# v of the gate by column blocks, u after it, and a sum with relu in one VectorE instruction

## Chip, cores and metric

One Trainium2 chip runs the same program on its 8 cores; each core computes one of the 8 sequences. There is no exchange between cores. The metric is the device time of the slowest core in microseconds (us), as a median over runs.

## What is computed

For each sequence x of 2048 positions with 1024 channels, two layers, each a token mixer and an MLP, each sub-layer followed by LayerNorm(alpha x + f(x)):

```
h = gelu(x @ w_in + b_in); u, v = h[..., :2048], h[..., 2048:]
v = layer_norm(v, v_g, v_b)                       # over 2048 channels
v = einsum('gts,bnsgc->bntgc', mask(w_s), v) + b_s  # 128 positions, 8 groups
mixer A = (u * v) @ w_out + b_out
mixer B = (b * causal_conv3(c * h)) @ w_out,  [b, c, h] = x @ w_in
MLP     = square(relu(x @ w1)) @ w2               # hidden 4096
```

Layer 0 uses mixer A, layer 1 mixer B.

## The kernel before

The sequence is done in two halves (h = 0, 1) of 1024 positions: eight token tiles (tt) of 128. For each half the stages are the gate (`gate_mixer`, mixer A), an MLP, `conv_mixer`, and a second MLP. `xres` holds the residual in fp32, `xT` the normalized input transposed in fp16, `H` 16 chunks of 128 hidden channels by 1024 positions. Weights are read as fp32 and cast to fp16 by the DMAs that GpSimd (POOL) issues: "ws" buffers (8, one block of 1024 x 128) and "wq" buffers (17, 512 x 512 each). SyncE (SP) issues x, rows of constants, transposes and the output.

In the gate, u comes out transposed (channels on partitions) in 16 blocks `u_block(fc, tb)` of eight matmuls for each 512 positions (L440), with the bias in ACT's gelu (L869). v comes out with positions on partitions: `v_tile(tt)` makes four products of 512 channels (`gemm_T`, L582), each ended by a ninth matmul that adds the bias from a small table `gc` (L585), then gelu (L906), statistics (L908), the reciprocal root on POOL, the normalization on ACT (L918) and the gain (L924, on POOL or VectorE). `sgu(tt)` mixes: ACT copies a bias into a bank (L932), four matmuls of 128 x 128 add the mixed v (L939), VectorE multiplies with u into H (L946). The order is: eleven u blocks, the tables (`init_gate`), v of tile 0, five u blocks, then v of tile tt + 1 with the mixing of tile tt. Then w_out is loaded into eight wq buffers, the first two token tiles are multiplied plainly, and the rest goes through `strassen_T`, a two by two block scheme with seven products, whose weight sums (`block_sums`, L411) take six more buffers.

`strassen_F` does the same for the first MLP product: 13 groups in each MLP call, six further blocks of a call's first half are plain or halved. Of a group's four results two are in PSUM banks, and two are the sum of a bank f and an fp32 tile ("k2" pool, VectorE L512). `square` then takes the relu on ACT into a k2 tile (L1043) and the square from there into H on VectorE (L1048) or ACT (L1049).

The order on each engine is made ahead by a planner (`Prog.schedule`): every operation has an engine or two, a duration and a program position; at each step the planner takes for each engine the operation that can start first (position decides within 0.05 us) and of these the earliest. Buffers of a pool are given in program order. Of a paced DMA it counts the bytes issued and lets at most 1.6 MB be under way: the DMA that moves the window gets waits on those that fell out of it. VectorE, ACT, POOL and SP run their lists strictly in order.

Of the kernel before, what the change touches and what calls it, by code (L numbers as in the profile page):

```python
# [8 lines left out]
FH = mybir.dt.float16  # L9
# [16 lines left out]
PATIENCE = 0.8  # L26
DMA_WINDOW = 1.6e6
# [18 lines left out]
class Prog:  # L46
# [60 lines left out]
    def schedule(self):  # L107
# [15 lines left out]

        def offer(op):
            for e in op.either or (op.eng,):
                cand[e].append(op)
# [6 lines left out]
        issued, total, low = [], 0, 0  # L133
        done = 0

        def start_of(op, e):
            t = max(op.ready, eng_free[e])
            if op.is_dma and op.paced:
                j = low
# [13 lines left out]
        while done < len(ops):  # L153
            best = None
            for e in ENGINES:
# [15 lines left out]
                if best is None or key < best[0]:  # L171
                    best = (key, e, op)
            assert best is not None, "no operation can start: a pool is held"
# [41 lines left out]
            for u in op.users:  # L215
                u.nleft -= 1
                lat = SEM_LAT if u.eng != op.eng or op.is_dma or u.either else 0.08
                u.ready = max(u.ready, op.end + lat)
                if u.nleft == 0:
                    offer(u)  # L220
# [122 lines left out]
def build_nc():  # L343
    nc = bass.Bass("TRN2", target_bir_lowering=False, dynamic_dma_scratch_size=4096)
# [14 lines left out]
    with es:  # L359
# [126 lines left out]
        def strassen_F(w, S, epilogue):  # L486
# [19 lines left out]
            epilogue(0, 0, a, True)  # L506
            for s, last in ((v, False), (u, True)):
                if last:
                    prod(b, W(w1, 1), SX(2), False)
                    epilogue(1, 0, b, True)  # L510
# [63 lines left out]
        def gemm_T(tt, wqs, hchunks=True, bias_q=None, gc=None):  # L574
            bk = vt("ps")
            A = H if hchunks else xT
            nk = 4 * len(wqs)

            def mm(e):
                ins = None  # L580
                for kc in range(nk):
                    ins = e.matmul(bk.buf[:], A[:, kc, tt * 128:(tt + 1) * 128], wqs[kc // 4].buf[:, kc % 4, :],  # L582
                                   start=(kc == 0), stop=(kc == nk - 1 and bias_q is None))
                if bias_q is not None:
                    ins = e.matmul(bk.buf[:], gc.buf[:, 1, bias_q * 128:(bias_q + 1) * 128], gc.buf[:, 0, :],  # L585
                                   start=False, stop=True)
                return ins
            rd = list(wqs) + ([("H", kc, tt) for kc in range(nk)] if hchunks else [("xT", tt, c) for c in range(8)])
            if bias_q is not None:
                rd += [(gc, 0), (gc, 1)]  # L590
            add("pe", mm, reads=rd, writes=[bk], dur=(nk + (bias_q is not None)) * T_MM)
            return bk

        def transpose_pe(xb, tt, gb=None):
            for q in range(2):
# [31 lines left out]
                add("act", None, reads=[bk, "gbT"], writes=wr, either={"act": (on_act, 1.55), "dve": (on_dve, 1.2)})  # L627

        def transpose_tiles(xbs, t0, gb=None):
# [8 lines left out]
            for q in range(2):  # L638
# [8 lines left out]
                def affine_act(e, q=q):  # L647
# [6 lines left out]
                    either={"act": (affine_act, 4 * (0.2 + n * 0.107)), "dve": (affine, 4 * (0.07 + n * 0.04))})  # L654
# [100 lines left out]
        def load_x(h, tt):  # L755
            r0 = (h * NT + tt) * 128
            add("sp", lambda e: e.dma_start(out=xres[:, tt, :], in_=x_ap[r0:r0 + 128, :]),
                writes=[(("xres", tt), 0), (("xres", tt), 1)], dma=("xr", tt), nbytes=128 * 4096, dur=0.06,
                paced=h > 0 or tt >= 4)
# [26 lines left out]
        def init():  # L786
# [12 lines left out]
            gc = vt("wt")  # L799
            clear_gc(gc)  # L800
# [3 lines left out]
            for bk in [vt("ps") for i in range(8)]:  # L804
                for i in range(2):
                    add("pe", lambda e, bk=bk: e.matmul(bk.buf[:], ones_bf[:], gc.buf[:, 0, :], start=True, stop=True),
                        reads=["ones", (gc, 0)], writes=[bk], dur=0.43)
            return gc

        def clear_gc(gc):  # L810
            add("dve", lambda e: e.memset(gc.buf[:, 0, :], 0.0), writes=[(gc, 0)], dur=0.3)

        def init_gate(gc):
# [4 lines left out]
            hi, lo, b = vt("k2"), vt("k2"), vt("k2")  # L818
            add("sp", lambda e: e.dma_start(out=b.buf[0:8, :], in_=bass.AP(rows_d, 9 * 1024, [[512, 4], [0, 2], [1, 512]])),
                writes=[b], dma=("c3", gc.seq), nbytes=16384, dur=0.06)  # L820
            add("dve", lambda e: e.tensor_copy(gc.buf[0:8, 0, :], b.buf[0:8, :]), reads=[b], writes=[(gc, 0)], dur=0.4)
            add("dve", lambda e: e.tensor_copy(hi.buf[0:8, :], gc.buf[0:8, 0, :]), reads=[(gc, 0)], writes=[hi], dur=0.4)
            add("dve", lambda e: e.tensor_tensor(lo.buf[0:8, :], b.buf[0:8, :], hi.buf[0:8, :], op=ALU.subtract),
                reads=[hi, b], writes=[lo], dur=0.7)
            add("dve", lambda e: e.tensor_tensor(hi.buf[0:8, :], hi.buf[0:8, :], lo.buf[0:8, :], op=ALU.subtract),
                reads=[hi, lo], writes=[hi], dur=0.7)
# [320 lines left out]
```

## Time and profile before

| | |
|---|---|
| median of 3 runs | 1458.36 us (1454.5 to 1460.49) |
| the profiled execution | 1464.58 us |
| its span on the slowest core (core 4) | 1463.0 us; all cores 1429.4 to 1463.0 |
| TensorE matmul (PE) | 1403.1 us busy, 96% |
| VectorE (DVE) | 1069.8 us, 73% |
| ScalarE (ACT) | 702.4 us, 48% |
| GpSimd (POOL) | 240.9 us, 16% |
| the chain that ended last | PE 71%, DMA 16%, issue 4%, ACT 4%, DVE 3% |

The profile follows one execution. "L440" is a line of the kernel. Matmuls are pipelined, so the busy time of one is longer than what it takes of PE's stream; the distance from one start to the next shows that. Idle time is put down to what ended it.

### The profile page before, as it was taken

The numbers are of one execution on the slowest core, as the hardware profiler recorded it, in microseconds if no ns is written. First come the engines' busy times: TensorE is split into PE (matmuls) and PEld (weight loads), VectorE is DVE, ScalarE is ACT, GpSimd is POOL, SyncE is SP. The second block draws the span as 40 slices with busy tenths as digits, with TensorE's granted clock in tenths as the row PEclk, the third lists the DMA queues.
The fourth block names the chain that finished last, engine by engine and source line by source line (L and its number), as shares of the span: only waits on it lengthen the run. The fifth ranks groups of instructions, "written<-read, shape, count | busy, mean of one in ns | idle before, by whom it ended". The sixth has DMA issues, their size and how long they took to land.

```text
span 1463.0 us, 23273 instructions; the slowest of 8 cores (1429.4 to 1463.0 us)
## 1 busy us (share of the span) xinstructions
PE 1403.1 (96%) x6988; PEld 665.9 (46%) x6988; DVE 1069.8 (73%) x2055; ACT 702.4 (48%) x1221; POOL 240.9 (16%) x422
## 2 busy tenths in 40 slices
PE   7999999998999998999998999999999999999996
PEld 3444445443446444443443444454444644544443
DVE  3257877887788677967681679779687876788777
ACT  2347457426463276336343574671474424751642
POOL 1125212111001101112011242121120111111100
PEclk7999999999999999999999999999999999999999
DMA  8999027856526739678988951293883364775702
GB/s 182 138 135 146 1 44 122 138 88 108 93 45 87 110 59 142 94 120 126 133 175 199 186 79 15 44 153 64 147 133 69 63 110 80 118 121 83 120 1 115
DMA packets 101138, 153.14 MB, mean 105 GB/s; under 512 B 52744, under 2 KB 52744, under 8 KB 101016
## 3 DMA queue, kind: packets, MB, share of 16 engines
q0 software_dynamic: 46608, 112.74, 50.6%
q1 hardware_dynamic: 54408, 38.91, 11.8%
q8 instruction: 59, 0.97, 0.3%
q14 instruction: 63, 0.52, 0.1%
HBM read 244.42 MB, written 8.39 MB: 173 GB/s over the span
## 4 chain that ended last, share of the span: by engine, by line
PE 71%; DMA 16%; issue 4%; ACT 4%; DVE 3%; POOL 1%; SPq 0%; DVEq 0%; POOLq 0%; ACTq 0%
PE ps L454 44%; PE ps L440 17%; PE ps L582 8%; DMA wq<-wbig 8%; DMA ws<-wsm 4%; DMA xT<-xb 2%; ACT xb L673 1%; ACT xT L650 1%; DMA wq<-x 1%; PE ps L939 1%; DMA xres<-x 1%; DMA sc<-rows 1%; DMA wt<-wsT 1%; PE ps L585 1%; ACT ps L932 1%
## 5 line engine op out<-in xcount | busy, mean ns | idle before, releaser
L440 PE MATMUL ps<-xT,ws 128*128 128x512 f16 (+1 forms) x2000 | 371.7, 347 | 7.4 <-DMA ws<-wsm 4.4
L440 PEld LDWEIGHTS ps<-xT,ws 128*128 128x128 f16 x2000 | 195.4, 98 | 178.0 <-issue 20.5
L454 PE MATMUL ps<-wq,sc 128*128 128x512 f16 x1184 | 271.6, 380 | 4.2 <-DVE xres L746 4.1
L454 PE MATMUL ps<-wq,H 128*128 128x512 f16 x888 | 207.5, 380 | 1.2 <-DVE xres L746 0.9
L398 POOL DMA_DIRECT2D ws<-wsm x208 | 110.6, 532 | 495.0 <-PE ps L440 183.5
L454 PEld LDWEIGHTS ps<-wq,sc 128*128 128x128 f16 x1184 | 115.8, 98 | 144.7 <-issue 6.3
L749 DVE SCALAR_TENSOR_TENSOR xres<-xres,ps 128x512 f32<-128x512 f32 x192 | 129.7, 684 | 50.4 <-PE ps L454 38.4
L454 PE MATMUL ps<-xT,ws 128*128 128x512 f16 x624 | 155.1, 381 | 3.0 <-DMA ws<-wsm 2.0
L407 ACT ACTIVATE ps<-ps 128x512 f32<-128x512 f32 x89 | 52.0, 584 | 180.1 <-PE ps L454 112.4
L454 PEld LDWEIGHTS ps<-wq,H 128*128 128x128 f16 x888 | 86.9, 98 | 107.4 <-issue 4.0
L398 POOL DMA_DIRECT2D wq<-wbig x104 | 55.8, 537 | 445.1 <-DMA wq<-wbig 156.5
L582 PE MATMUL ps<-wq,xT 128*128 128x512 f16 x512 | 122.5, 383 | 2.4 <-DMA wq<-wbig 2.4
L454 PE MATMUL ps<-wq,wt 128*128 128x512 f16 x416 | 107.5, 381 | 4.6 <-DVE wt L411 3.4
L411 DVE TENSOR_TENSOR wq<-wq 128x2048 f16<-128x2048 f16 x80 | 96.0, 1218 | 12.0 <-DMA wq<-wbig 11.6
L582 PE MATMUL ps<-wq,H 128*128 128x512 f16 x448 | 100.3, 384 | 0.3
L454 PEld LDWEIGHTS ps<-xT,ws 128*128 128x128 f16 x624 | 60.4, 98 | 79.0 <-issue 9.8
L673 ACT ACTIVATE xb<-xres,st 128x1024 bf16<-128x1024 f32 x48 | 54.7, 1141 | 61.7 <-DVE st L670 52.6
L582 PEld LDWEIGHTS ps<-wq,xT 128*128 128x128 f16 x512 | 49.5, 99 | 59.2 <-issue 4.9
L746 DVE TENSOR_TENSOR xres<-xres,ps 128x512 f32<-128x512 f32 x74 | 50.6, 685 | 30.9 <-PE ps L454 30.7
L869 ACT ACTIVATE H<-ps,cols_sb 128x512 f16<-128x512 f32 x64 | 43.1, 685 | 59.6 <-PE ps L440 59.6
L582 PEld LDWEIGHTS ps<-wq,H 128*128 128x128 f16 x448 | 43.8, 99 | 53.1 <-issue 3.0
L454 PEld LDWEIGHTS ps<-wq,wt 128*128 128x128 f16 x416 | 40.5, 98 | 55.0 <-issue 8.5
(159 smaller groups left out, 1798.0 us busy)
## 6 DMA issues: line engine op xcount, KB each, us to landing
ws<-wsm POOLq DMA_DIRECT2D x208, 256.0 KB, 5.5
wq<-wbig POOLq DMA_DIRECT2D x104, 512.0 KB, 7.4
lnc<-rows SPq DMA_DIRECT2D x20, 512.0 KB, 8.7
xres<-x SPq DMA_DIRECT2D x16, 512.0 KB, 7.4
out<-sc SPq DMA_DIRECT2D x15, 512.0 KB, 3.2
wq<-x POOLq DMA_DIRECT2D x3, 512.0 KB, 11.0
sc<-rows POOLq DMA_DIRECT2D x2, 512.0 KB, 9.2
xT<-xb SPq DMA_TRANSPOSE x38, 3.2
```

What stands on the lines that cost most here:

```text
L398: add("pool", lambda e: e.dma_start(out=dst(), in_=src), writes=w, dma=stream, nbytes=nbytes, dur=0.55)
L407: add("act", lambda e: e.activation(out=dst.buf[:], in_=src.buf[:], func=AF.Copy), reads=[src], writes=w, dur=t_act(512))
L411: add("dve", lambda e: e.tensor_tensor(out(), a(), b(), op=op), reads=reads, writes=writes, dur=t_dve(n, True))
L440: ins = e.matmul(bk.buf[:, p * n * 128:(p + 1) * n * 128], ws.buf[:, kc, :], xT[:, kc, t0 * 128:(t0 + n) * 128], start=(kc == 0 and not be ...
L454: ins = e.matmul(bk.buf[:], lhs(kc), rhs(kc), start=(first and kc == 0), stop=(kc == nk - 1), skip_group_check=True)
L582: ins = e.matmul(bk.buf[:], A[:, kc, tt * 128:(tt + 1) * 128], wqs[kc // 4].buf[:, kc % 4, :], start=(kc == 0), stop=(kc == nk - 1 and bia ...
L585: ins = e.matmul(bk.buf[:], gc.buf[:, 1, bias_q * 128:(bias_q + 1) * 128], gc.buf[:, 0, :], start=False, stop=True)
L650: ins = e.activation(out=x, in_=x, func=AF.Identity, scale=gbT[:, gb, c:c + 1], bias=gbT[:, 4 + gb, c:c + 1])
L673: add("act", lambda e: e.activation(out=junk.buf.bitcast(mybir.dt.bfloat16)[:, 0:D], in_=z, func=AF.Square, bias=s.buf[:, 24:25], accum_ou ...
L746: add("dve", lambda e: e.tensor_tensor(xres[:, tt, sl], xres[:, tt, sl], bk.buf[:], op=ALU.add), reads=[bk, k], writes=[k], dur=t_dve(512))
L749: add("dve", lambda e: e.scalar_tensor_tensor(out=xres[:, tt, sl], in0=xres[:, tt, sl], scalar=ALPHA if alpha else 1.0, in1=bk.buf[:], op0 ...
L869: add("act", lambda e: e.activation(out=H[:, fc, tb * 512:(tb + 1) * 512], in_=bk.buf[:], func=AF.Gelu, bias=cols[:, fc:fc + 1]), reads=fu ...
```

## The change

The gate is written anew. v is made by column blocks (cb) of 512 channels, each over all eight token tiles, before u; its results stay in eight wq buffers. The bias is copied by ACT from a row (one broadcast DMA on SP for each column block) into the bank, and the eight matmuls add to it. With the fourth column block, the first eight half blocks of u are interleaved and each tile is normalized in three VectorE instructions (one tensor_scalar, two multiplies by the gain). The rest of u follows, with one mixing step of four chunks behind each half block. The table `gc` goes.

```diff
+            def v_block(cb, tt):
+                bk, row, o = vt("ps"), rows[cb // 2], cb % 2 * 512
+                add("act", lambda e: e.activation(out=bk.buf[:], in_=row.buf[:, o:o + 512], func=AF.Copy),
+                    reads=[(row, cb % 2), "warm"], writes=[bk], dur=t_act(512, True))
...
+                        ins = e.matmul(bk.buf[:], xT[:, kc, tt * 128:(tt + 1) * 128], av[cb][kc // 4].buf[:, kc % 4, :],
+                                       start=False, stop=(kc == 7), skip_group_check=True)
...
+            def v_norm(tt, vg):
...
+                rstd(s, lambda: s.buf[:, 25:26], 1.0, True)
+                add("dve", lambda e: e.tensor_scalar(v16(tt, 0, 2048), v16(tt, 0, 2048), s.buf[:, 24:25], s.buf[:, 26:27],
+                                                     op0=ALU.subtract, op1=ALU.mult),
...
+            if h == 0:
+                load_x(0, 0)
+            load_av(0)
+            if h == 0:
+                for tt in range(1, NT):
+                    load_x(0, tt)
+            load_av(1)
+            for tt in range(NT):
+                if tt == 4:
+                    load_av(2)
+                V.append(vt("wq"))
+                if h == 0:
+                    transpose_x(tt)
+                v_block(0, tt)
+            load_av(3)
+            for cb in (1, 2):
+                for tt in range(NT):
+                    v_block(cb, tt)
+            wsT, vg, bias2 = init_gate()
...
+            for tt in range(NT):
+                v_block(3, tt)
+                u_part(0, tt)
+                v_norm(tt, vg)
...
+            for q in range(1, 4):
+                for i in range(8):
+                    u_part(q, i)
+                    sgu(q - 1, i, wsT, bias2)
             ao = load_blocks(BIG_BASE["a_out"])
+            for tt in range(NT):
+                sgu(3, tt, wsT, bias2)
```

In `strassen_F` the add into the k2 tile goes; `square` takes the bank and the tile and makes relu of the sum in one custom VectorE instruction, max(min(a + b, 3e38), 0), straight into H; the other two results get their relu from ACT into H. The square is then taken in place.

```diff
-                add("dve", lambda e, s=s: e.tensor_tensor(s.buf[:], f.buf[:], s.buf[:], op=ALU.add),
-                    reads=[f, s], writes=[s], dur=t_dve(512))
-                epilogue(0 if last else 1, 1, s, False)
+                epilogue(0 if last else 1, 1, f, s)
...
+                            add("dve", lambda e: e._custom_dve(TENSOR_ADD_SAT, out=hs, in0=src.buf[:], in1=part.buf[:],
+                                                               s0=3e38, s1=0.0),
+                                reads=[src, part], writes=wr, dur=t_dve(512))
```

In the planner, of paced DMAs that could start within 0.7 us the one with the earliest program position goes first, and each queue gets the waits of the window for itself. Some assumed durations (the transposes' epilogues) are longer, the bias of w_out is added when VectorE has time (lazy), the first four x tiles are paced as the others, and the program is built by `bacc.Bacc` with `compile()` in place of `bass.Bass`.

```diff
+DMA_SLACK = 0.7
...
+            if best[2].is_dma and best[2].paced:
+                best = min((x for x in picks if x[2].is_dma and x[2].paced and x[0][0] <= best[0][0] + DMA_SLACK),
+                           key=lambda x: x[2].prio)
...
-                while op.paced and low < len(issued) and total - issued[low][0] > DMA_WINDOW:
-                    op.deps.setdefault(issued[low][1].idx, True)
-                    low += 1
+                while op.paced and low[e] < len(issued) and total - issued[low[e]][0] > DMA_WINDOW:
+                    op.deps.setdefault(issued[low[e]][1].idx, True)
+                    low[e] += 1
```

## Rows read from the trace of the kernel before

**Rows 1.** The page, busy us (share of the span) and instructions of each engine.

```profile
PE 1403.1 (96%) x6988; PEld 665.9 (46%) x6988; DVE 1069.8 (73%) x2055; ACT 702.4 (48%) x1221; POOL 240.9 (16%) x422
```

**Rows 2.** PE's waits, whole span: waiting <- waited for: us, times, longest.

```profile
PE ps L939 <- ACT ps L932: 8.9, 12, 2.1
...
PE ps L440 <- DMA ws<-wsm: 4.4, 2, 3.6
PE ps L454 <- DVE k_3 L512: 4.0, 1, 4.0
...
PE ps L582 <- DMA wq<-wbig: 2.4, 2, 1.9
...
PE ps L440 <- issue: 0.3, 2, 0.2
```

**Rows 3.** Groups by line, the ninth matmul: busy us, mean ns of one | idle before.

```profile
L585 PE MATMUL ps<-wt 128*128 128x512 f16 x64 | 24.3, 379 | 0.0
```

**Rows 4.** Time line of PE, 105 to 108: start, us, what, count.

```profile
105.34 1.89 PE L582 MATMUL ps<-wq,xT 128*128 128x512 f16 x8
107.06 0.38 PE L585 MATMUL ps<-wt 128*128 128x512 f16 x1
107.28 1.06 PE L939 MATMUL ps<-wt,sc 128*128 128x128 f16 x16
```

**Rows 5.** Time line of PE, two groups of matmuls behind L939 waits.

```profile
119.53 3.40 PE L582 MATMUL ps<-wq,xT 128*128 128x512 f16 x8
...
170.20 5.30 PE L582 MATMUL ps<-wq,H 128*128 128x512 f16 x16
```

**Rows 6.** Groups by line, ScalarE and VectorE.

```profile
L749 DVE SCALAR_TENSOR_TENSOR xres<-xres,ps 128x512 f32<-128x512 f32 x192 | 129.7, 684 | 50.4 <-PE ps L454 38.4 <-PE ps L582 9.7 <-DVE xres L684 0.5
...
L411 DVE TENSOR_TENSOR wq<-wq 128x2048 f16<-128x2048 f16 x80 | 96.0, 1218 | 12.0 <-DMA wq<-wbig 11.6
...
L946 DVE TENSOR_TENSOR H<-ps,H 128x512 f16<-128x512 f32 x64 | 41.4, 676 | 10.8 <-PE ps L939 10.8
...
L906 ACT ACTIVATE sc<-ps 128x512 f16<-128x512 f32 x64 | 36.9, 588 | 39.8 <-PE ps L585 38.1 <-DVE sc L843 1.7
L932 ACT ACTIVATE ps<-sc 128x512 f32<-128x512 f32 x64 | 36.0, 594 | 6.0 <-POOL sc L924 3.5 <-DVE sc L924 1.6 <-PE ps L939 0.8
...
L924 DVE TENSOR_TENSOR sc<-sc 128x512 f16<-128x512 f16 x32 | 29.3, 924 | 9.6 <-ACT sc L918 9.6
...
L723 DVE TENSOR_SCALAR xb<-xres,st 128x512 f16<-128x512 f32 x49 | 26.3, 544 | 2.3 <-DVE st L716 0.5
...
L512 DVE TENSOR_TENSOR k_2<-ps,k_2 128x512 f32<-128x512 f32 x24 | 16.5, 688 | 8.7 <-PE ps L454 4.2 <-ACT k_2 L407 4.1
...
L1043 ACT ACTIVATE k_3<-k_2 128x512 f16<-128x512 f32 x10 | 6.3, 626 | 1.8 <-DVE k_2 L512 1.7
```

**Rows 7.** Stretches of the start: us, busy by engine (instructions), PEclk, DMA share, GB/s.

```profile
0.00:18.36 18.36, 9.96 (x48) 5.04 (x49) 7.03 (x20) 4.47 (x7) 2.26 (x8) 0.77 0.79 182
0.00:40.00 40.00, 29.62 (x143) 13.98 (x144) 13.14 (x33) 11.34 (x18) 7.15 (x18) 0.79 0.83 173
40.00:64.50 24.50, 24.50 (x115) 11.05 (x114) 2.93 (x5) 9.62 (x14) 3.23 (x6) 1.00 0.96 140
```

**Rows 8.** Time line at the seam of the halves, with idle time and its end.

```profile
729.59 0.48 DVE L816 MEMSET wt<- 64x512 f16 x1 [5.01 <-DMA wt<-wsT]
...
732.72 2.78 PE L454 MATMUL ps<-wq,sc 128*128 128x512 f16 x8 [4.08 <-DVE xres L746]
...
788.62 5.07 PE L440 MATMUL ps<-xT,ws 128*128 128x512 f16 x16 [3.65 <-DMA ws<-wsm]
```

**Rows 9.** The page, DMA issues: count, KB each, us to landing.

```profile
lnc<-rows SPq DMA_DIRECT2D x20, 512.0 KB, 8.7
```

**Rows 10.** Line L398, weight loads issued by POOL: ns min/median/max.

```profile
L398 POOL DMA_DIRECT2D ws<-wsm x208: 527/527/662, 1.5 to 1380.5; - x104
```

**Rows 11.** VectorE's waits for block weights: us, times, longest.

```profile
DVE wq L411 <- DMA wq<-wbig: 11.6, 4, 6.1
```

More of the change, by code:

```diff
@@ L122, in schedule, with release @@
         cand = {e: [] for e in ENGINES}
+        def release(op, end):
+            for u in op.users:
+                u.nleft -= 1
+                lat = SEM_LAT if u.eng != op.eng or op.is_dma or u.either else 0.08
+                u.ready = max(u.ready, end + lat)
+                if u.nleft == 0:
+                    offer(u)
         def offer(op):
@@ L132, in schedule @@
         dma_free = 0.0
-        issued, total, low = [], 0, 0
+        issued, total, low = [], 0, {e: 0 for e in ENGINES}
         done = 0
@@ L138, in start_of @@
             if op.is_dma and op.paced:
-                j = low
+                j = low[e]
                 while j < len(issued) and total - issued[j][0] > DMA_WINDOW:
@@ L170, in schedule @@
                 key = (t, op.prio) if op.is_dma and op.paced else (t, -1)
-                if best is None or key < best[0]:
-                    best = (key, e, op)
-            assert best is not None, "no operation can start: a pool is held"
+                picks.append((key, e, op))
+            assert picks, "no operation can start: a pool is held"
+            best = min(picks, key=lambda x: x[0])
+            if best[2].is_dma and best[2].paced:
+                best = min((x for x in picks if x[2].is_dma and x[2].paced and x[0][0] <= best[0][0] + DMA_SLACK),
+                           key=lambda x: x[2].prio)
             (t, _), e, op = best
@@ L214, in schedule @@
                     free_at[v.pool].append((max(o.end for o in v.ops) + SEM_LAT, v.idx, tuple(v.ops)))
[L215 to L220, printed above, removed]
+            release(op, op.end)
         self.order = order
@@ L581, in mm @@
                 for kc in range(nk):
[L582 to L586, printed above, removed]
-                return ins
[L588 to L591, printed above, removed]
+                    ins = e.matmul(bk.buf[:], H[:, kc, tt * 128:(tt + 1) * 128], wqs[kc // 4].buf[:, kc % 4, :],
+                                   start=(kc == 0), stop=(kc == nk - 1))
+                return ins
+            add("pe", mm, reads=list(wqs) + [("H", kc, tt) for kc in range(nk)], writes=[bk], dur=nk * T_MM)
             return bk
@@ L805, in init, with init_gate @@
                 for i in range(2):
[L806 to L813, printed above, removed]
+                    add("pe", lambda e, bk=bk: e.matmul(bk.buf[:], ones_bf[:], zero.buf[:, 0, :], start=True, stop=True),
+                        reads=["ones", zero], writes=[bk, "warm"], dur=0.43)
+        def init_gate():
             wsT, vg, bias2 = vt("wt"), vt("sc"), [vt("sc"), vt("sc")]
@@ L872, in u_block, with sgu, mm @@
                     dur=t_act(512) + 0.1, table="gelu")
+            def sgu(q, tt, wsT, bias2):
+                bk = vt("ps")
+                hk = [("H", 4 * q + j, tt) for j in range(4)]
+                add("act", lambda e: e.activation(out=bk.buf[:], func=AF.Copy,
+                                                  in_=bias2[q // 2].buf[:, q % 2 * 512:(q % 2 + 1) * 512]),
+                    reads=[(V[tt], q)] + [(bias2[q // 2], c) for c in range(4 * q, 4 * q + 4)] + hk, writes=[bk],
+                    dur=t_act(512, True))
+                def mm(e):
+                    for j in range(4):
+                        c = 4 * q + j
+                        ins = e.matmul(bk.buf[:, j * 128:(j + 1) * 128], v16(tt, c * 128, (c + 1) * 128),
+                                       wsT.buf[:, c // 8, (c // 2 % 4) * 128:(c // 2 % 4 + 1) * 128],
+                                       start=False, stop=(j == 3), skip_group_check=True)
+                    return ins
+                add("pe", mm, reads=[(V[tt], q), wsT], writes=[bk], dur=0.27)
+                hs = H[:, 4 * q:4 * q + 4, tt * 128:(tt + 1) * 128]
+                add("dve", lambda e: e.tensor_tensor(hs, bk.buf[:].rearrange("p (c t) -> p c t", c=4), hs, op=ALU.mult),
+                    reads=[bk] + hk, writes=hk, dur=t_dve(512))
```

191 lines of the change are left out of this document (65 added, 126 removed).

## Prediction, made before the changed kernel was run

> **What bounds the kernel now.** The first view to read is the page's busy time by engine: matmuls of TensorE (PE) fill 1403.1 us, 96% of the span [rows 1]; no other engine passes 73%, as the table above shows. So the time falls by what PE no longer has to stream, and by those of its 60 idle us that go; work taken from the other engines counts only through these two. The second view is the list of PE's waits [rows 2]. The mixing matmul (L939) waits 8.9 us for ScalarE's bias copy (L932), products wait 4.4 us for u weights, 4.0 us for a bank that VectorE had not emptied (L512), 2.4 us for v weights. "Issue" is 0.3 us in all: PE's own instruction stream costs nothing. The third view, the time line, shows one more wait of 4.08 us, for a residual, at 732.72 [rows 8].
>
> A wait has a second price. Behind some, the granted clock is at its lower level, 1.2 GHz, and the same matmuls take longer: after L939 waits, eight took 3.40 us where 1.89 is normal, and sixteen 5.30 us [rows 4, 5]. I count 1.6 us for such a dip.
>
> **The change part by part.** The sum is made against the profiled execution, 1464.6 us, whose span is 1463.0. That is 6.2 us above the median shown, 1458.4; I take the same difference for the median.
>
> *v bias.* Before, each of 64 v products ends in a ninth matmul (L585) [rows 3]. The time line shows its price without the overlap that the busy column hides: eight matmuls start at 105.34, the ninth at 107.06, the next group at 107.28, so it takes 0.22 us of PE [rows 4]. 64 x 0.22 = 14.1: **-14**, in PE's stream, where nothing hides it. In its place an ACT copy into the bank goes ahead of the products, of the form of L932, 0.594 us. A v product takes PE 1.72 us; ACT's copy and gelu (L906, 0.588) take 1.18 [rows 6], so ACT can run ahead over the eight banks. What a late copy costs is rival 1.
>
> *Start.* Before, four x tiles and a u weight block opened the kernel; now one x tile, a bias row (256 KB) and two v blocks (512 KB each as written) must land before the first product. From 40 to 64.5 us casting loads held the DMA engines at 96% and moved 140 GB/s as written, 146 at a full share; in the first 18.36 us, mostly x without a cast, it was 182 at 0.79, which is 230 [rows 7]. So x0 takes 2.3 us, the row 1.1, the v pair 7.2: with 2 us before the first issue, about 13 us. The other seven x tiles add 16, less what ran beside (27 to 29 us), row and v blocks of the second column 8.3 (35 to 37). PE does the first column (64 matmuls) as x comes in, waits 4 us or more, and is free of loads from then on: a column takes it 8 x 1.72 = 13.8 us, its weights 8.3. By 40 us it has done 16 + 64 + 64 matmuls and, behind a dip, some 17 of the second column, against 143 before. 18 x 0.215: **-4**. If the loads are a seventh slower, the second column starts at 40 us and nothing is won; a quarter slower costs 4. u blocks in the gap would win its 4 us and the dip besides. Bounds -9 to +4.
>
> *Mixing.* Now a u block (1.72 us of PE) stands between two mixing steps and v's normalization is over before, so neither the copy nor the gate product on VectorE is urgent. What goes: 8.9 us (L939), two dips (3.2), and 2.4 us for v weights, now loaded columns ahead: 14.5. The last column's eight mixing steps have no u block between them; each needs 0.594 of ACT and 0.676 of VectorE (L946) against 0.22 of PE, partly beside the first output products. I leave 1.7 us there in each half: **-11**. Bounds -15 to 0 (the waits only move).
>
> The multiply by v's gain (L924), which POOL and VectorE share and where VectorE needs 924 ns for 512 elements, 32 times, moves to VectorE alone in pieces of 1024: some 0.7 us each, between L512's 0.688 for 512 in fp32 and 1.218 for 2048 in fp16 (L411) [rows 6]. One tensor_scalar over 2048 replaces ACT's normalization; the trace has none of that size. Four times L723 (0.544 for 512 from fp32) is the upper end, 2.2 us, one L723 the lower. I take 1.0, nearest to L411's 1.218 for 2048 elements with two inputs. VectorE gets 16 x (1.4 + 1.0) = 38 us where L924 took it 29, in 16 steps of 3.4 us: hidden.
>
> *Seam between the halves.* At 729.59 VectorE comes out of a wait of 5.01 us for the mixing matrix (L816). Residuals stand behind it, their banks stay full, PE waits 4.08 us and then runs eight matmuls in 2.78 us; at 788.62 it waits 3.65 us for a u block and then runs sixteen in 5.07 [rows 8]. With 1.6 for each dip some 11 us hang on these two. The matrix is now asked for after three columns of v, and the u blocks after it. New: the first v products need two "wq" buffers while the output weights of the half before hold 14 of 17, and a bias row in an "sc" buffer that a finished tile must leave first; rows take 8.7 us to land [rows 9]. u blocks, whose buffers are free, can go ahead. I count +4: **-7**. Bounds -11 to +4.
>
> *Sum and relu in one.* 13 groups in each of four calls with two sums each: 104. ACT loses 104 x 0.63 = 65 us (L1043 from a "k" tile). VectorE keeps an add of the same shape: L512 takes 0.688, L749, with two operations, 0.684, so I take 0.69 [rows 6]. The result goes straight to H. PE gains only from shorter chains to a bank, and VectorE's lateness before the 4.0 us at L512 came from a DMA (rival 4), which stays. **-2**; bounds -6 to +7 (104 x 0.07).
>
> *Buffers at the gate's end.* v lives in eight of 17 "wq" buffers until its last mixing step. The output weights need eight, their sums six more, the x sums three. So the block sums (L411, eight of 1.218 us) can't start before the last column's mixing, when VectorE also has 8 x 0.676 and the residuals. Four plain output products give 14 us of cover (64 matmuls). I take 3 us in each half: **+6**; bounds 0 to +16.
>
> *Load order and waits.* The planner now prefers the load that is older in the program within 0.7 us, each queue keeps the window for itself, and the program goes through another builder. Cost 0; PE's 0.3 us of issue leave little to win; bounds -3 to +8.
>
> Sum: -14 - 4 - 11 - 7 - 2 + 6 = -32. 1464.6 - 32 = 1432.6 profiled, **1426 us** for the median.
>
> **A rule against the change.** POOL issued the u weights' loads in 527 ns at the median and 662 at most, 208 times, while VectorE ran its tensor_scalars (L723) [rows 6, 10]. The Trainium skill ("SBUF — State Buffer", section "SBUF: two separate sides") says that VectorE in a two-port mode locks GpSimd out, so that such a load's descriptors come late. The trace shows no such delay; rival 3 is what it would do here.
>
> **Rivals.**
> 1. *The preload becomes the wait.* The mixing steps waited 12 times for such a copy, 0.74 us each [rows 2], of 64. If the 64 v products do likewise, +9: 1435. Against it: ACT has 0.5 us to spare per product.
> 2. *Stalls move, they don't vanish.* Only the bias matmuls count: -14, 1444. For it: each wait stands where a planned time was missed, and the new plan will miss others.
> 3. *Late issues.* Sixteen tensor_scalars each hold one load up by 1.0 us, and each delay ends in a PE wait: +16, 1442. Against it: u blocks are loaded ahead by then.
> 4. *Slower: the window starves the block weights.* The window's wait used to be put on one load, of whichever queue; now each queue gets it. If that holds the block weights back at the eight w2 stages and two output stages, each costs what was paid once before: VectorE, waiting for a block, stands before the add that frees a bank: 4.0 us of PE (L512) and a dip of 1.6. Ten stages: +56 against -32, 1482; from six on the gain is gone. For it: 11.6 us of VectorE's waits are of this kind [rows 11]. Against it: SyncE issues few loads (20 of rows [rows 9]), so POOL's queue carried nearly all window waits already.
> 5. *Nothing is left*: start and seam at their upper bounds and the buffers too, +4 + 4 + 16, against -14, -11 and -2: 1455.
>
> **How the numbers follow.** Forecast 0.55 (its own range 1406 to 1433), rival 1 0.15, rival 2 0.12, rival 3 0.03, rival 5 0.08, rival 4 0.07. Range 1406 to 1449: the low end has mixing, seam, start and sums at their lower bounds and no new wait for buffers (-14 - 15 - 11 - 9 - 6 = -55, of which I allow -52), the high end takes in rivals 1 to 3 and 5 us of spread. Faster by over 0.5% (7 us, about what a measurement can tell from no change): the forecast, rivals 1 to 3 and a little of rival 5, 0.87; same 0.07; slower 0.06.
>
> **What would show it.** No L585 group, PE's busy time down by 14, its waits on the mixing below 4 us. The first v product near 13 us, the second column near 36. The sum-and-relu rows at 0.69 us; over 1.5 us VectorE would bound the MLP stages. Wrong would be: PE waits for the preload over 9 us, waits at the first block products behind the gate over 10 us, or VectorE waiting longer for block weights than 11.6 us.

## The result and the profile after

The changed kernel takes 1410.55 us at the median of four runs where the kernel before took 1459.42 beside it. The ratio is 0.9653, 95% interval 0.9596 to 0.9709: 50 us less. In some executions the cores of one die show a lower granted clock and the time is longer (1537.75 us in one of these four, 1402.42 to 1413.83 in the others); the ratios leave such executions out, the medians in us do not, and on one chip, named below, every execution was of this kind. The profiled execution took 1413.83, with a span of 1412.1 on core 3 (all cores 1396.8 to 1412.1). The forecast was 1426, 32 us less: the time lies in its range, near the low end, and the gain is some 18 us larger than forecast.

The page after: instructions in the span, busy us of each engine, the chain that ended last.

```profile
span 1412.1 us, 18834 instructions; the slowest of 8 cores (1396.8 to 1412.1 us)
PE 1370.1 (97%) x6924; PEld 657.6 (47%) x6924; DVE 1039.9 (74%) x1972; ACT 679.7 (48%) x1211; POOL 208.3 (15%) x390
PE 91%; DMA 4%; DVE 2%; ACT 1%; issue 1%; POOL 0%; SPq 0%; POOLq 0%; DVEq 0%; ACTq 0%
```

PE lost 64 matmuls, as planned, but 33 us of busy time, more than twice their price. And the program has 4439 instructions fewer (23273 before), while the engines' counts [rows 1] fall by only some 250, weight loads among them: most of what went does no arithmetic at all. That was the clue to the largest gain that a single edit gives below.

PE's and VectorE's waits after (us in total, times, longest), answering to [rows 2] and [rows 11].

```profile
PE ps L463 <- DVE xres L749: 6.3, 1, 6.3
PE ps L601 <- DVE xb L764: 6.2, 1, 6.2
PE ps L861 <- DMA wq<-wbig: 5.4, 1, 5.4
PE ps L601 <- ACT xT L610: 3.1, 4, 0.8
PE ps L463 <- DVE sc L420: 2.3, 1, 2.3
PE ps L861 <- ACT xT L610: 2.1, 3, 0.7
...
DVE wt L420 <- DMA ws<-wsm: 11.7, 7, 3.4
...
DVE wq L420 <- DMA wq<-wbig: 0.2, 1, 0.2
```

No wait for the mixing (L904) is left here, and none for the preload of the bias into a bank (L856) has come. All waits at L601 and L861 lie in the start, L749 and `sc L420` at the seam. Between these two places PE hardly idles.

Groups after, by form: shape, count, busy us, mean ns, idle time before.

```profile
L904 PE MATMUL ps<-wt,wq 128*128 128x128 f16 x256 | 22.8, 219 | 0.0
L856 ACT ACTIVATE ps<-sc 128x512 f32<-128x512 f32 x64 | 37.3, 600 | 5.0 <-PE ps L805 2.1 <-DVE sc L822 1.7
L882 DVE TENSOR_TENSOR wq<-wq,sc 128x1024 f16<-128x1024 f16 x32 | 20.1, 679 | 0.0
L1036 DVE CUSTOM_DVE_ANT_0 H<-ps,k_2 128x512 f16<-128x512 f32 x26 | 17.9, 687 | 17.5 <-ACT k_2 L416 17.4
L877 DVE TENSOR_SCALAR wq<-wq,st 128x2048 f16<-128x2048 f16 x16 | 12.9, 807 | 6.1 <-POOL st L660 5.5
```

The durations of the new operations came close: the bias copy 0.600 (taken 0.594), the gain 0.679 for 1024 (0.7), sum and relu 0.687 (0.69), the tensor_scalar over 2048 elements 0.807 (1.0).

The start is the one stage that got worse. PE in the first 18.36 and 40 us (its busy us and matmuls stand first; then weight loads, VectorE, ScalarE, POOL, granted clock, DMA share, GB/s), against [rows 7]:

```profile
0.00:18.36 18.36, 7.42 (x24) 2.93 (x24) 1.66 (x8) 5.74 (x10) 1.76 (x7) 0.81 0.67 125
0.00:40.00 40.00, 22.20 (x108) 10.07 (x109) 9.79 (x26) 15.52 (x28) 4.16 (x11) 0.83 0.74 177
```

By 40 us PE has done 108 matmuls, 143 before. SyncE's queue, POOL's second load and PE in that stretch:

```profile
1.73 0.42 SPq L757 DMA_DIRECT2D xres<-x  x1
2.19 0.43 SPq L847 DMA_DIRECT2D sc<-rows  x1
...
11.17 0.59 POOL L407 DMA_DIRECT2D wq<-wbig  x1 [8.79 <-DMA xres<-x]
...
11.38 0.80 SPq L757 DMA_DIRECT2D xres<-x  x2
...
20.60 3.57 PE L861 MATMUL ps<-wq,xT 128*128 128x512 f16 x8 [5.40 <-DMA wq<-wbig]
23.96 0.63 PE L601 MATMUL ps<-ident,xb 128*128 128x128 f16 x4
25.38 0.38 PE L601 MATMUL ps<-ident,xb 128*128 128x128 f16 x4 [0.78 <-ACT xT L610]
26.45 1.90 PE L861 MATMUL ps<-wq,xT 128*128 128x512 f16 x8 [0.69 <-ACT xT L610]
```

After the first x tile and the row SyncE issues nothing for nine microseconds, and POOL issues the second v block at 11.17 only, behind the landing of the first x tile: the window. That block lands at 20.50, and the first v product starts at 20.60. Then a second limit shows. Products follow each other at 26.45, 30.42 and 34.40, every 3.97 us, for a product of 1.7 us: four transposes, ScalarE's copy, four more, another copy, the product. VectorE's casts of these tiles, which come ahead of the transposes, waited for PE by then and not for a load; the chain itself is the limit.

### The profile page after: what moved, and what is told of

Its sections match the earlier page's. It is cut to its first block, busy times and chain, and to the rows that moved or that the text cites. A ratio compares the mean times of both kernels' runs of the same rounds, so it can differ in the third digit from the quotient of the medians.

```text
span 1412.1 us, 18834 instructions; the slowest of 8 cores (1396.8 to 1412.1 us)
## 1 busy us (share of the span) xinstructions
PE 1370.1 (97%) x6924; PEld 657.6 (47%) x6924; DVE 1039.9 (74%) x1972; ACT 679.7 (48%) x1211; POOL 208.3 (15%) x390
## 4 chain that ended last, share of the span: by engine, by line
PE 91%; DMA 4%; DVE 2%; ACT 1%; issue 1%; POOL 0%; SPq 0%; POOLq 0%; DVEq 0%; ACTq 0%
PE ps L463 52%; PE ps L449 24%; PE ps L861 8%; PE ps L588 6%; DMA wq<-wbig 1%; DMA out<-sc 1%; PE ps L904 1%; DMA xres<-x 1%; PE ps L601 1%; DMA ws<-wsm 0%; DMA xT<-xb 0%; DVE sc L700 0%; DVE xres L749 0%; ACT xT L610 0%; ACT sc L673 0%
## 5 line engine op out<-in xcount | busy, mean ns | idle before, releaser
L449 PEld LDWEIGHTS ps<-xT,ws 128*128 128x128 f16 x2000 | 193.1, 98 | 158.3 <-issue 3.7
L463 PE MATMUL ps<-wq,H 128*128 128x512 f16 x888 | 205.9, 379 | 0.0
L749 DVE SCALAR_TENSOR_TENSOR xres<-xres,ps 128x512 f32<-128x512 f32 x192 | 129.9, 684 | 58.7 <-PE ps L463 43.4
L463 PEld LDWEIGHTS ps<-wq,H 128*128 128x128 f16 x888 | 86.7, 98 | 104.5 <-DVE xres L746 0.4
L1044 ACT ACTIVATE H<-H 128x512 f16<-128x512 f16 x187 | 116.6, 630 | 28.7 <-DVE H L1036 25.8
L861 PE MATMUL ps<-wq,xT 128*128 128x512 f16 x512 | 115.0, 383 | 7.6 <-DMA wq<-wbig 5.4
L1040 ACT ACTIVATE H<-ps 128x512 f16<-128x512 f32 x152 | 89.0, 592 | 48.1 <-PE ps L463 36.9
L588 PE MATMUL ps<-wq,H 128*128 128x512 f16 x448 | 98.0, 379 | 0.0
L420 DVE TENSOR_TENSOR wq<-wq 128x2048 f16<-128x2048 f16 x80 | 95.7, 1217 | 1.0 <-PE ps L463 0.7
L463 PEld LDWEIGHTS ps<-xT,ws 128*128 128x128 f16 x624 | 59.5, 98 | 73.8 <-ACT ps L416 2.1
L861 PEld LDWEIGHTS ps<-wq,xT 128*128 128x128 f16 x512 | 49.9, 98 | 68.2 <-issue 7.6
L868 DVE BATCH_NORM_STATS2 st<-wq 128x6 f32<-128x512 f16 x64 | 43.3, 688 | 33.9 <-ACT wq L866 33.8
```

What stands on the lines that cost most here:

```text
L420: add("dve", lambda e: e.tensor_tensor(out(), a(), b(), op=op), reads=reads, writes=writes, dur=t_dve(n, True))
L449: ins = e.matmul(bk.buf[:, p * n * 128:(p + 1) * n * 128], ws.buf[:, kc, :], xT[:, kc, t0 * 128:(t0 + n) * 128], start=(kc == 0 and not be ...
L463: ins = e.matmul(bk.buf[:], lhs(kc), rhs(kc), start=(first and kc == 0), stop=(kc == nk - 1), skip_group_check=True)
L588: ins = e.matmul(bk.buf[:], H[:, kc, tt * 128:(tt + 1) * 128], wqs[kc // 4].buf[:, kc % 4, :], start=(kc == 0), stop=(kc == nk - 1))
L749: add("dve", lambda e: e.scalar_tensor_tensor(out=xres[:, tt, sl], in0=xres[:, tt, sl], scalar=ALPHA if alpha else 1.0, in1=bk.buf[:], op0 ...
L861: ins = e.matmul(bk.buf[:], xT[:, kc, tt * 128:(tt + 1) * 128], av[cb][kc // 4].buf[:, kc % 4, :], start=False, stop=(kc == 7), skip_group ...
```

## The experiments

Three explanations stood against each other: the gate's new order gives the gain; the planner's load order gives it; or the other builder does, which the prediction had put at nothing. Ratios are to the kernel before on the same chip (1456.22 us for the first four).

**The builder alone** in the kernel before:

```diff
-    nc = bass.Bass("TRN2", target_bir_lowering=False, dynamic_dma_scratch_size=4096)
+    nc = bacc.Bacc("TRN2", target_bir_lowering=False, dynamic_dma_scratch_size=4096)
...
+    nc.compile()
     return nc
```

> The kernel before with one edit: the other builder and its compile step. The changed kernel gained about 50 us where 32 were forecast, and nearly all of PE's idle time outside the gate went with it, about 20 to 25 us on the slowest core. Theory 1 (the load order removed it) and theory 2 (sum and relu in one removed it) both expect no change here: 1459 us within 5. Theory 3 (the builder, which left 18834 instructions of 23273, removed it by taking away waits that stood as instructions of their own) expects some 1437 us, with the same PE busy time and fewer instructions.

Measured: 1424.08 us, ratio 0.9782 (0.9747 to 0.9817), 32 us less where theory 3 had expected some 22, with the same operations in the same order on each engine (but for four memsets in a wider type, and one that changes places with its neighbour). Its page:

```profile
span 1422.0 us, 19017 instructions; the slowest of 8 cores (1414.7 to 1422.0 us)
PE 1386.5 (98%) x6988; PEld 664.3 (47%) x6988; DVE 1068.8 (75%) x2055; ACT 702.0 (49%) x1221; POOL 243.5 (17%) x422
```

PE's waits in it:

```profile
PE ps L605 <- DVE xb L769: 7.3, 6, 2.7
PE ps L444 <- DMA ws<-wsm: 4.4, 1, 4.4
...
PE ps L943 <- ACT ps L936: 1.8, 4, 0.8
```

The counts of the five engines equal [rows 1] and 4256 other instructions are gone. The mixing's wait, 8.9 us in [rows 2], is 1.8 here without any change to the mixing. PE's busy time falls by 16.6 us with no matmul less, in part because there are fewer waits behind which the clock drops [rows 5]: the slowest core's mean granted clock is 0.990, where it was 0.985. By my estimate that is some 8 us (0.015 of 1463 less 0.010 of 1422); the rest of the 16.6 is open. At the median of the eight cores PE's idle time (gaps over 0.15 us) falls by 17.5 us and its busy time by 13.4, which together make up the 32. What went are separate wait instructions: on VectorE, ScalarE, PE and POOL the trace before has 1946, 1371, 1160 and 805 of them, this one 334, 286, 261 and 283; the other waits are carried by the instruction that needs them. One chain shows what a handoff cost, from VectorE's aggregate over POOL's two steps to ScalarE's normalization (start, duration). Before:

```profile
152.62 0.27 DVE L910 BATCH_NORM_AGGREGATE st<-st 128x2 f32<-128x24 f32 x1
...
153.05 1.16 POOL L658 TENSOR_SCALAR st<-st 128x1 f32<-128x1 f32 x1 [3.79 <-DVE st L910]
...
154.36 0.55 POOL L660 TENSOR_TENSOR st<-st,neghalf 128x1 f32<-128x1 f32 x1
...
155.01 0.16 DVE L913 SCALAR_TENSOR_TENSOR st<-st 128x1 f32<-128x1 f32 x1 [0.85 <-POOL st L660]
...
155.32 1.24 ACT L918 ACTIVATE sc<-sc,st 128x1024 f16<-128x1024 f16 x1 [2.45 <-DVE st L913]
```

With the other builder:

```profile
151.32 0.25 DVE L914 BATCH_NORM_AGGREGATE st<-st 128x2 f32<-128x24 f32 x1
...
151.65 0.32 POOL L662 TENSOR_SCALAR st<-st 128x1 f32<-128x1 f32 x1 [3.85 <-DVE st L914]
...
152.05 0.73 POOL L664 TENSOR_TENSOR st<-st,neghalf 128x1 f32<-128x1 f32 x1
...
152.82 0.16 DVE L917 SCALAR_TENSOR_TENSOR st<-st 128x1 f32<-128x1 f32 x1
...
153.06 2.37 ACT L922 ACTIVATE sc<-sc,st 128x1024 f16<-128x1024 f16 x2 [3.17 <-DVE st L917]
```

The gaps from an end to the next start are 0.16, 0.15, 0.10 and 0.15 us before, 0.08, 0.08, 0.04 and 0.08 here. (That POOL's first step took 1.16 us in the one and 0.32 in the other is not the builder's doing: its medians are 0.190 and 0.192.) Over the whole traces, from the release to the start of the instruction that waited for it, medians worked out from the semaphore events (ns):

| kernel | VectorE | ScalarE | PE | POOL's load behind a landing |
|---|---|---|---|---|
| before | 93 | 83 | 136 | 547 |
| builder alone | 24 | 23 | 42 to 46 | 285 |
| changed kernel | 24 | 23 | 43 to 56 | 297 |

**The changed kernel with the old load order** (one window for all queues, no preference for the older load):

```diff
-                while op.paced and low[e] < len(issued) and total - issued[low[e]][0] > DMA_WINDOW:
+                while op.paced and low < len(issued) and total - issued[low][0] > DMA_WINDOW:
...
-                best = min((x for x in picks if x[2].is_dma and x[2].paced and x[0][0] <= best[0][0] + DMA_SLACK),
-                           key=lambda x: x[2].prio)
```

> The changed kernel with the planner's old rules for loads: earliest start first, and one window whose wait goes to a single load. Theory 1 (the load order removed the idle time outside the gate): 20 us or more slower than the changed kernel, about 1430 us, with VectorE waiting for block weights (wq) 10 us or more and PE waits of 2 to 4 us behind them. Theories 2 and 3: within 5 us of the changed kernel, 1405 to 1413 us. My prediction put this edit at 0 with bounds of -3 to +8.

Measured: 1431.44, ratio 0.9824 (0.9792 to 0.9857): 25 us of the gain go, as theory 1 had it. Its waits:

```profile
PE ps L857 <- ACT ps L852: 7.1, 1, 7.1
...
PE ps L459 <- DVE wt L416: 4.1, 2, 2.6
...
DVE wq L416 <- DMA wq<-wbig: 12.4, 4, 5.5
```

Here, with the bias row late, the preload is a wait once, and the block weights are late as in [rows 11]; no wait of PE names them, so how much of the 25 us they cost is not shown. What the new order is worth, put at 0, is 25 us with the new gate.

**The changed kernel with the old sum and relu** (VectorE's add into a k2 tile, ScalarE's relu, then the square):

```diff
-                epilogue(0 if last else 1, 1, f, s)
+                add("dve", lambda e, s=s: e.tensor_tensor(s.buf[:], f.buf[:], s.buf[:], op=ALU.add),
+                    reads=[f, s], writes=[s], dur=t_dve(512))
+                epilogue(0 if last else 1, 1, s, False)
```

> The changed kernel with the old sum: VectorE adds into a k2 tile, ACT takes the relu from there into another k2 tile, and the square goes from there to H. Theory 2 (the shorter chain and the freed k2 tiles removed the idle time in the MLP stages): 15 to 20 us slower than the changed kernel, about 1425 us, with PE waits for banks held by the add. Theory 1 and my prediction (2 us, bounds -6 to +7): 1407 to 1413 us.

Measured: 1418.38, ratio 0.974 (0.9707 to 0.9772), some 13 us slower than the change by the ratios; the two intervals just touch, so the size is uncertain. It lies between the two expectations. The waits that theory 2 named are not there: on none of the eight cores does a wait of PE name the add. At the mean of the cores PE waits 4.1 us for residuals (1.7 with the change), 1.9 for weights in "ws" buffers and 1.9 for a copy of transposes (none with the change). How the old sum leads to these is open.

**The changed kernel with the old gate** (`gate_mixer`, `gemm_T`, the tables and the free first x tiles of before; new load order, sum and relu, builder):

```diff
-            def v_block(cb, tt):
+            def v_tile(tt):
...
+                if bias_q is not None:
+                    ins = e.matmul(bk.buf[:], gc.buf[:, 1, bias_q * 128:(bias_q + 1) * 128], gc.buf[:, 0, :],
+                                   start=False, stop=True)
```

> The changed kernel with the gate of before (v by token tiles with the ninth matmul, the old start, the old order of u); load order, sum with relu and builder as changed. The new gate is worth 14 us of bias matmuls, 12 us of waits around the mixing and some 8 us at the seam, less what the new start costs (some 6 us more idle before 45 us): 25 to 30 us, so about 1437 us. If the waits in the gate were a matter of load order as well, only the 14 less 6 would show: about 1418 us.

Measured: 1424.75, ratio 0.9781 (0.9751 to 0.9811): 19 us above the changed kernel by the ratios, between the two expectations, and no better than the builder alone. Its page:

```profile
PE 1386.0 (97%) x6988; PEld 665.0 (47%) x6988; DVE 1048.1 (74%) x1989; ACT 679.3 (48%) x1181; POOL 244.4 (17%) x422
```

and its wait for the mixing:

```profile
PE ps L946 <- ACT ps L939: 5.1, 5, 3.2
```

To see where the parts act, I took from all eight cores the time at which the last layer norm of a half's stage ends, and the median over the cores (us of each stage, one execution per kernel):

| kernel | gate 1 | MLP | conv | MLP | gate 2 | MLP | conv | MLP | sum |
|---|---|---|---|---|---|---|---|---|---|
| before | 223.0 | 207.6 | 114.8 | 198.9 | 192.0 | 196.8 | 119.5 | 190.2 | 1442.7 |
| builder alone | 211.5 | 200.6 | 115.3 | 193.4 | 187.6 | 196.3 | 116.1 | 188.7 | 1409.5 |
| old gate | 215.2 | 200.6 | 114.1 | 190.6 | 187.5 | 199.6 | 114.1 | 187.7 | 1409.6 |
| changed | 209.6 | 200.9 | 114.0 | 191.0 | 172.2 | 200.9 | 114.1 | 187.7 | 1390.5 |

The builder gives 24 of its 33 us in the first half. The new gate gives 15.3 in the second half and 5.6 in the first, where it has the start against it. Load order with sum and relu win some 7 us in the conv stages and in the two last MLPs of a half, and with the old gate give them back in the first gate and the second half's first MLP. By the same measure the changed kernel with the old load order has a sum of 1407.1, 16.6 above the changed kernel, 11.9 of it in the first half; the 25 us of the ratios are those of the slowest core.

**Separate waits put back.** If the separate waits are what the old builder cost, they must cost it again. In the builder-alone kernel each wait of some engines is asked for twice, so that one of the two stands as an instruction of its own; nothing else changes.

```diff
-                if kind == "dma":
-                    eng.wait_ge(sem_dma[a], b)
-                else:
-                    eng.wait_ge(sem_eng[a.eng], a.sig_val)
+                for _ in range(2 if name in ("dve","act") else 1):
+                    if kind == "dma":
+                        eng.wait_ge(sem_dma[a], b)
+                    else:
+                        eng.wait_ge(sem_eng[a.eng], a.sig_val)
```

The first two ran on the one chip that the section on the result speaks of: 1484.35 and 1482.3 us there, where the kernel before took 1489.73, and nothing follows from them.

> The kernel before with the other builder (1424 us), but every wait on VectorE and ScalarE is asked for twice, so that a first wait stands as an instruction of its own again: 1946 on VectorE and 1371 on ScalarE, as many as in the kernel before (334 and 286 with the builder alone). POOL, SP and PE keep their waits inside the instructions. Theory 3a (what the builder saves is the start of VectorE's and ScalarE's instructions behind a wait, about 90 ns before against 24 ns, in chains that PE waits for): most of the 32 us come back, 1445 to 1456 us. Theory 3b (it is the loads, issued sooner by POOL and SP): 1424 us within 4.

> The same with the waits of POOL and SP apart (805 and 177 separate waits, against 283 and 63); VectorE, ScalarE and PE keep theirs inside. Theory 3b (loads go out sooner, a load issued behind a landing starts 285 ns after it in place of 547, so fewer blocks come late): 1440 us or more. Theory 3a: 1424 us within 4.

Both were run again on another chip (before: 1457.81), with PE's waits as a third (`("pool","sp")` and `("pe",)` in the line above).

> The kernel with the other builder and the waits of VectorE and ScalarE apart, once more: in the first run of it one die ran at a lower clock throughout, which decides nothing. Theory 3a (the start of VectorE's and ScalarE's instructions behind a wait): 1440 to 1456 us. Theory 3b (the loads, issued sooner): 1424 us within 4.

> The same with the waits of POOL and SP apart, once more. Theory 3b: 1440 us or more. Theory 3a: 1424 us within 4.

> The same with the waits of PE apart (1160 separate waits, against 261). Behind a wait PE began 136 ns after the release before, and its weight load 42 ns after it with the builder; with some 90 visible waits that is 8 us at the most. PE's own idle time put down to issue was 0.3 us, so by the prediction's reading it is 1424 us within 4; if the waits in PE's stream matter, 1428 to 1434 us. If the three classes together don't give back the 32 us of the builder, something else in it counts.

| separate waits on | us | ratio (95%) | over the builder alone |
|---|---|---|---|
| VectorE, ScalarE | 1445.85 | 0.991 (0.9867 to 0.9954) | +19 |
| POOL, SyncE | 1439.24 | 0.9842 (0.9717 to 0.9968) | +9 |
| PE | 1433.95 | 0.9827 (0.9732 to 0.9922) | +7 |

The last column is the difference of the ratios, 0.9782 for the builder alone, times 1457. The handoff medians move as they should and only where they should: with VectorE and ScalarE apart 92 and 82 ns again and POOL's 285; with POOL's apart 529 and VectorE's 24; with PE's apart 104 to 135. The first kernel's span by the page, and PE's wait for the mixing in it:

```profile
span 1443.9 us, 21714 instructions; the slowest of 8 cores (1424.8 to 1443.9 us)
```

```profile
PE ps L944 <- ACT ps L937: 7.2, 9, 1.6
```

The same wait with POOL's and SyncE's waits apart:

```profile
PE ps L944 <- ACT ps L937: 6.6, 10, 1.3
```

The first has 2697 instructions more than the builder alone, 1612 on VectorE and 1085 on ScalarE, and the wait of the mixing for ScalarE is back (7.2, against 1.8). Its interval lies clear of the builder alone's, so it is shown that VectorE's and ScalarE's separate waits cost time; the middle value, 19, is over half of the 32 us, but by the two intervals it can be 10 to 27. The time is what theory 3a expected. With POOL's and SyncE's waits apart it lies between the two theories, and the mixing waits nearly as long; POOL's two steps stand in the chain above. The three sum to some 34; that the second and third have a share is likely, but their intervals overlap that of the builder alone. By the sums of the stage table they are 1427.7, 1422.3 and 1413.3, that is 18, 13 and 4 over the builder alone, in one execution each. The builder was not taken out of the changed kernel: what it is worth there is not measured.

**The start and the seam.** In the changed kernel the first x tile, bias row and v pair were taken out of the window's waits, alone and then together with the second half's x loads put off until the second v column is done.

```diff
-                writes=[(("xres", tt), 0), (("xres", tt), 1)], dma=("xr", tt), nbytes=128 * 4096, dur=0.06)
+                writes=[(("xres", tt), 0), (("xres", tt), 1)], dma=("xr", tt), nbytes=128 * 4096, dur=0.06, paced=h > 0 or tt > 0)
...
-                av[cb] = [load_wq(BIG_BASE["a_v"] + cb // 2, (cb % 2) * 2 + i) for i in range(2)]
+                av[cb] = [load_wq(BIG_BASE["a_v"] + cb // 2, (cb % 2) * 2 + i, h > 0 or cb > 0) for i in range(2)]
...
-                    load_x(h, tt)
+                    load_x(h, tt, [(V[tt], 1)])
```

> The changed kernel with the first x tile, the first bias row and the two v blocks of the first column taken out of the load window, so that they go out at once. In the changed kernel the second v block was issued only at 11.2 us, behind the landing of the first load (10.6), and the first v product began at 20.6 where I had forecast 13. If the window is what holds the start, the first v product begins at 13 to 15 us and 4 to 6 us are gained, about 1403 us. If the bandwidth is the limit, it stays near 20 us and nothing is gained: 1408.

> The changed kernel, with the x loads of the second half made to wait for the tile's second v product. In its profile, PE waited 6.3 us at 712 for a residual, behind ScalarE, which had waited for an output DMA that stood on SP behind an x load held by the window. If that is the cause, the wait goes, with its stretch at the lower clock: 5 to 8 us on the cores that had it (two of eight), so the slowest core and the time fall by 3 to 6 us, 1403 us. If not: 1408 within 4.

Each edit by itself ran on that same chip (1475.84 and 1482.21 us), and nothing follows from them either. Together, on the other:

> The changed kernel with both repairs: the first loads outside the window, and the x loads of the second half behind the tile's second v product. The seam's repair removes the 6.3 us wait and its dip on the cores that had it, the start gains 1 to 4 us (first v product near 16 us in place of 20.6). Together 3 to 8 us: 1400 to 1405 us, faster than both kernels. If seam and start are given back elsewhere: 1408 within 4.

Measured: 1411.8, ratio 0.9676 (0.9602 to 0.9749), the same as the change, as expected if start and seam are given back elsewhere. PE in its start (the time line):

```profile
16.13 3.39 PE L861 MATMUL ps<-wq,xT 128*128 128x512 f16 x8 [2.31 <-ACT xT L610]
```

and its waits, whole span:

```profile
PE ps L463 <- DVE xres L746: 4.0, 1, 4.0
PE ps L449 <- DVE H L910: 3.1, 3, 1.4
```

The first product starts 4.5 us earlier, behind ScalarE's copy of the transposes and no longer behind a load, so the window did hold it; but the next ones again stand 4 us apart. The residual's wait of 6.3 us is 4.0, and a new one has come at L910. By the table's measure the first gate is 2.3 us shorter (207.3) and the second 5.0 longer (177.2). No version better than the changed kernel was found.

## Why the prediction came out as it did

The time fell into the range because errors offset in part. The terms of the gate (-14, -4, -11, -7, +6) made -30; taking the new gate alone away costs 19. The builder was put at 0 and is worth 32 in the kernel before. That the low end of the range, 1406, reached far enough is luck: it was made from mixing, seam, start and sums at their lower bounds, and the start, for one, went the other way.

- **Load order and waits, 0 with bounds -3 to +8: the step that failed.** The sentence was "PE's 0.3 us of issue leave little to win". It looked for the cost of waits on the engine that bounds, in the row that is named for it [rows 2]. But VectorE and ScalarE lost 60 to 70 ns at each handoff (93 against 24, 83 against 23) and POOL 260 at a load, and PE met that as lateness of others: of L932 above all (at the mean of the cores 8.0 us before, 2.0 with the builder). Its own separate waits cost the least of the three groups, 7 us, which is not clear of nothing. The page before had the trace of it: 23273 instructions, of which the five engines' work makes under 18000. The load order itself is not 0 either; it is worth 25 us with the new gate and nothing to be measured, together with sum and relu, with the old one. Why these parts join up so is open; the stage table only shows where the gain is given back.
- **v bias, -14: right.** L585 is gone, 6988 matmuls became 6924, and against the old gate PE's busy time falls by 15.9, in which the clock behind fewer waits has a share.
- **Start, -4 with bounds -9 to +4: wrong sign.** Forecast were the first v product at 13 us and the second column at 36; they came at 20.60 and, by the semaphores that PE waits for, at 42.40, though that column's weights had landed by 38.28. The step counted the bytes of the loads and took the queues as free; that the first x tiles were now paced like all others stood in the change, and I did not follow what the window would do to the second v block. And "as x comes in" took the loads for the limit of the first column, where transposes and ScalarE's copies are, at 3.97 us a tile. In the first 80 us PE is not busy for 15.1 to 19.2 us on the eight cores, 9.5 to 13.9 before: about +6.
- **Mixing, -11: the waits went as said (8.9 to none),** but most of that the builder alone also gives (8.9 to 1.8); only one of the two can be credited with it. The cause I named was ScalarE's copy asked for too late. In the plan of before it is the handoffs for the most part: at the mean of the cores 8.0 us are 2.0 with the builder, and 8.0 or 6.6 again with the separate waits of VectorE and ScalarE or of POOL and SyncE. The plan has a share too: the old gate under the new load order waits 4.8 in spite of the builder, the new gate not at all.
- **Seam and buffers, -7 and +6.** With bias and mixing halved, the second gate was forecast at -7 - 5.5 - 7 + 3 = -16.5; against the old gate it is -15.3, against before -19.8. The size is right; the parts are not measured one by one. No wait for buffers is seen at the first output products, which were taken at +3 each half. At the seam a wait of 6.3 us remains on core 3, which is the slowest core, and of the others only core 1 has one like it. VectorE and ScalarE wait there for the output that must leave an "sc" buffer, in a queue where x loads of the second half come between:

```profile
703.82 0.69 DVE L420 TENSOR_TENSOR sc<-H 128x1024 f16<-128x1024 f16 x1 [4.71 <-DMA out<-sc]
708.95 0.33 SPq L757 DMA_DIRECT2D xres<-x  x1
709.33 0.42 SPq L709 DMA_DIRECT2D out<-sc  x1
715.71 1.15 ACT L673 ACTIVATE sc<-xres,st 128x1024 bf16<-128x1024 f32 x1 [24.23 <-DMA out<-sc]
719.17 3.60 PE L463 MATMUL ps<-wq,sc 128*128 128x512 f16 x8 [6.28 <-DVE xres L749]
```

In the run above that put the x loads off, this wait became smaller and another grew: the cause named here is not shown.
- **Sum and relu, -2 with bounds -6 to +7.** The duration was right (0.687), the worth about -13 by the ratios: mis-sized, and by that middle value outside its bounds. The step said that PE gains only through shorter chains to a bank; with the old sum put back PE waits for no such chain, so the way in which the 13 us come about was not the one named, and it is open. In the stage table the old form adds 2.4 us to each conv stage and 1.9 and 3.0 to the MLPs of the first half (its row would read 210.3, 202.8, 116.5, 194.0, 172.9, 200.7, 116.4, 187.8).
- **The rivals.** The preload never waits (1), though with the old load order it does once. Late issues (3) do come, but small: POOL's loads take 537 ns at the median, and the 64 that ran beside a new tensor_scalar (L877) on the eight cores 717 at the mean and up to 1094. In the lines below two tensor_scalars stand as one row, the second from 91.41 to 92.22; the load's issue, begun at 91.43, ends at 92.34, 0.12 us after it. That agrees with the Trainium skill ("SBUF — State Buffer", section "SBUF: two separate sides"), by which VectorE in a two-port mode keeps GpSimd from writing a load's descriptors. No wait of PE follows from it: after the start none names a load. So the rival had the mechanism and not the size, some 0.2 us six to ten times on a core, where it took 1.0 sixteen times. Block weights are waited for 0.2 us where it was 11.6 (4): the window by queue does the opposite of what that rival feared.

```profile
90.45 1.77 DVE L877 TENSOR_SCALAR wq<-wq,st 128x2048 f16<-128x2048 f16 x2 [0.80 <-POOL st L660]
...
91.43 0.91 POOL L407 DMA_DIRECT2D wq<-wbig  x1
```

## What to carry to other kernels

When the page's instruction count far exceeds the engines' work, ask what the rest is: separate waits delay every handoff of the engines that feed the bounding one, and appear there as waits for those engines; here its own issue showed 0.3 us. Of a change that makes loads paced, follow the window from the first load on, and of a first stage cost the chain per tile as well as the bytes. Try the smallest edit of a change alone before crediting the large one with the gain.

## What the runs showed of the hardware

A wait carried in the instruction against one standing ahead of it: release to start 24 against 93 ns on VectorE, 23 against 83 on ScalarE, 42 to 46 against 136 on PE, and 285 against 547 for POOL's load behind a landing. A custom VectorE instruction with two inputs, one in PSUM, and a clamp takes 687 ns for 128x512, as long as the plain add (0.688, [rows 6]). Matmuls that add to a bank which ScalarE filled with the bias take 383 ns busy each at L861, as the v products did before at L582 (383), so PE shows no price for the fill. A load that POOL issues beside a tensor_scalar of 128x2048 in fp16 takes 717 ns to issue at the mean, against 537 at the median of all.
